# A hybrid two-block network on one core: a new order in the attention loop, a narrow normalizer and a new order in the matrix recurrences

## What is computed

```python
# mLSTM, per head: t queries, s keys
scores = einsum("tk,sk->ts", q, k) * exp(dmat - m_row)        # causal
h = (scores @ v) / maximum(abs(sum(scores, -1)), exp(-m_row)) # the normalizer
y = group_norm(h * sigmoid(og), center=True)
# SSD
y = (einsum("ln,sn,ls,sp->lp", cc, bc, lmat, xc) + xs * d_skip) * silu(z)
y = group_norm(y, 1, norm_g, center=False)
```

```python
s = einsum('qhcd,khcd->hcqk', q, k)           # two maps c per head, over 512 keys
p = softmax(s, axis=-1)
da = einsum('hqk,khv->qhv', p[:, 0] - lam * p[:, 1], v)
mx = einsum('hqm,mhd->qhd', softmax(einsum('qhd,mhd->hqm', q * 128 ** -0.5, mk)), mv)
```

## Time and profile before

| | before |
|---|---|
| median of 3 runs | 3386.85 us (3380.41 to 6549.61) |
| profiled execution | 3385.07 us, span 3383.4 us |
| instructions | 49933 |
| PE busy | 3254.1 us (96%) |
| PE weight loads | 2589.0 us (77%) |
| DVE busy | 2475.9 us (73%) |
| ACT busy | 1902.0 us (56%) |
| POOL busy | 242.4 us (7%) |
| DMA | 600.28 MB, mean 177 GB/s |

### The profile page before, as it was taken

How to read it: one execution, slowest core, us unless ns; L and a number is a source line. 1 busy time by engine, 2 the same in 40 slices (tenths; PEclk the granted TensorE clock), 3 DMA queues, 4 the chain that set the end, 5 groups by cost and what they waited for, 6 DMA issues and landing times. The chain is left out here.

```text
span 3383.4 us, 49933 instructions
## 1 busy us (share of the span) xinstructions
PE 3254.1 (96%) x19234; PEld 2589.0 (77%) x19234; DVE 2475.9 (73%) x2843; ACT 1902.0 (56%) x2145; POOL 242.4 (7%) x202
## 2 busy tenths in 40 slices
PE   8998799999999999999999998999999999899998
PEld 6876467888888888888767776788887877678886
DVE  6745759999999999999668866566536886666543
ACT  4315337777777787787547546354316635544422
POOL 0000001212212122122000000000000000000000
PEclk9999899999999999999999999999999999999999
DMA  4103259999999999999512210222322221122331
GB/s 148 64 26 109 69 206 362 371 369 364 373 360 366 374 366 360 374 360 374 205 47 89 70 60 19 85 87 94 107 92 72 73 66 42 47 84 94 100 102 67
DMA packets 118964, 600.28 MB, mean 177 GB/s; under 512 B 20738, under 2 KB 24338, under 8 KB 68402
## 3 DMA queue, kind: packets, MB, share of 16 engines
q1 hardware_dynamic: 105490, 580.64, 47.0%
q0 software_dynamic: 13312, 17.35, 2.1%
HBM read 585.77 MB, written 28.90 MB: 182 GB/s over the span
## 5 line engine op out<-in xcount | busy, mean ns | idle before, releaser
L2614 DVE TENSOR_TENSOR wl<-raw,wh 128x2048 fp32r<-128x2048 f32 x384 | 872.5, 2286 | 52.4 <-ACT wh L2543 52.4
L2543 ACT ACTIVATE wh<-raw 128x2048 fp32r<-128x2048 f32 x384 | 735.7, 1916 | 190.9 <-PE pu L2484 143.9
L2482 PE MATMUL pu<-wh,Xh 128*128 128x512 f32 x1024 | 409.7, 400 | 0.0
L2483 PE MATMUL pu<-wl,Xh 128*128 128x512 f32 x1024 | 399.7, 390 | 0.0
L2484 PE MATMUL pu<-wh,Xl 128*128 128x512 f32 x1024 | 399.2, 390 | 0.0
L4469 ACT ACTIVATE w_high<-w_raw 128x1024 fp32r<-128x1024 f32 (+1 forms) x114 | 131.2, 1151 | 319.7 <-PE acc L4441 161.1
L4516 DVE TENSOR_TENSOR w_low<-w_raw,w_high 128x1024 fp32r<-128x1024 f32 (+1 forms) x114 | 152.4, 1337 | 185.1 <-PE ps L4399 99.8
L4421 PE MATMUL ps<-x_high,w_high 128*128 128x512 f32 x656 | 255.2, 389 | 0.0
L4422 PE MATMUL ps<-x_low,w_high 128*128 128x512 f32 x656 | 255.2, 389 | 0.0
L2482 PEld LDWEIGHTS pu<-wh,Xh 128*128 128x128 f32 x1024 | 192.3, 188 | 45.6 <-issue 7.9
L2484 PEld LDWEIGHTS pu<-wh,Xl 128*128 128x128 f32 x1024 | 192.3, 188 | 42.6
(11 more groups left out here) (836 smaller groups left out, 6535.9 us busy)
## 6 DMA issues: line engine op xcount, KB each, us to landing
raw<-in_exp_w SPq DMA_DIRECT2D x384, 1024.0 KB, 7.7
w_raw<-in_w_in SPq DMA_DIRECT2D x100, 512.0 KB, 3.3
w_raw<-in_w_up SPq DMA_DIRECT2D x82, 512.0 KB, 3.7
w_raw<-in_w_down SPq DMA_DIRECT2D x32, 704.0 KB, 4.0
w_raw<-in_w_out SPq DMA_DIRECT2D x32, 384.0 KB, 3.1
kv_raw<-in_w_mem_kv SPq DMA_DIRECT2D x16, 512.0 KB, 3.7
x<-in_x SPq DMA_DIRECT2D x4, 1024.0 KB, 8.4
w_raw<-in_w_out SPq DMA_DIRECT2D x8, 512.0 KB, 4.4
```

Of the source, the lines that this page charges most:

```text
L2482: nc.tensor.matmul(o, lh[:, k, :], wh[:, m % PARTS, c], start=(m >= 8 and kh == 0 and kk == 0), stop=False)
L2483: nc.tensor.matmul(o, lh[:, k, :], wl[:, m % PARTS, c], start=False, stop=False)
L2543: nc.scalar.activation(wh[:, m % PARTS, :], raw[:, m % RAW, :], ACT.Copy).then_inc(w_high, 1)
L2614: nc.vector.tensor_tensor(wl[:, m % PARTS, :], raw[:, m % RAW, :], wh[:, m % PARTS, :], ALU.subtract).then_inc(w_low, 1)
```

## The change

It has three parts.

1. *Normalizer.* The denominators are no longer repeated over 64 partitions. `half_ones` (GpSimd makes it at the stage's start) has ones in 16 of its 48 columns; a matmul of 32 columns for each head and block of queries c puts the denominators of both heads of a pair in the partitions 32 c to 32 c + 31 of bank 0, 128 tokens wide. The bounds get the same form early (`m_bounds`, behind the first scores). ScalarE's absolute value, VectorE's maximum and its reciprocal then go over 256 elements a partition, and TensorE spreads the reciprocal over heads (`m_over`, `m_shared`) behind the first SSD sum.
2. *Order in the recurrences.* `m_rows(1)` goes ahead of the scores and sums of its step, the GLA spread ahead of the sums, `s_rows(0)` ahead of the last two sums, and in SSD step 2 the mean and `s_rows(1)` ahead of memory tile 12. Tiles 11 and 12 use bank 5. The last gate is done in halves.
3. *Attention loop.* On TensorE `scores(n + 2)` comes first, then `turn`, `mem_scores(n + 2)`, `mem_turn`, and the tile after them. `sums` writes `x_var` (first quarter) and `mem_sums` its second quarter, so `turn` waits for the gather of the step before and not for its store. One semaphore serves both sums. The scale of the scores moves into the copies that make the queries, and two small VectorE instructions a step go.

```diff
-        dn = K.sb(ctx, "dn", [P, 2, S])
+        dn = K.sb(ctx, "dn", [P, 2, P])
+        half_ones = K.sb(ctx, "half_ones", [P, 48])
+        bound_rows = K.sb(ctx, "bound_rows", [P, 2, 32])
-        kv_bank = lambda t: B[:, {10: 5, 13: 2, 14: 2, 15: 3}.get(t, 1), 0:MEM]
+        kv_bank = lambda t: B[:, {10: 5, 11: 5, 12: 5, 13: 2, 14: 2, 15: 3}.get(t, 1), 0:MEM]
...
                     for e in (0, 1):
-                        o = slice(64 * e, 64 * e + 64)
-                        mm = nc.tensor.matmul(B[o, p, j * P:S], K.c("ones", P, 0, 64), atts[q % 2][:, e, j * P:S],
-                                              start=(j == 0), stop=(j == NT - 1))
+                        for c in range(j, NT):
+                            mm = nc.tensor.matmul(B[32 * c:32 * c + 32, 0, p * P:(p + 1) * P], half_ones[:, 16 - 16 * e:48 - 16 * e],
+                                                  atts[q % 2][:, e, L[c]], start=(j == 0 and e == 0), stop=(j == c and e == 1),
+                                                  skip_group_check=True)
...
+                m_bounds()
                 for q in range(LAST):
...
+                    if q == NT - 2:
+                        m_rows(1)
                     if q + 1 < LAST:
                         m_scores(q + 1)
+                    if q == NT - 1:
+                        pe.wait_ge(l_inverse, 1)
+                        pe.wait_ge(memory.taken, MEM_TILES + 2)
+                        head_spread(B[:, 3, :], 0).then_inc(l_spread, 1)
+                        head_spread(B[:, 1, :], 1).then_inc(l_spread, 1)
+                    if q == LAST - 2:
+                        s_rows(0)
                     m_sums(q)
-                    if q == NT - 2:
-                        m_rows(1)
...
-                s_rows(0)
...
-                pe.wait_ge(m_abs, 1)
-                pe.wait_ge(em_out, 1)
-                for h in range(H):
-                    o = slice(64 * (h % 2), 64 * (h % 2) + 64)
-                    mm = nc.tensor.matmul(B[o, h // 2, :], row_of(ROW_I, h, 64), rows, start=True, stop=True)
-                mm.then_inc(em_spread, 1)
                 for q in range(LAST):
                     if q == NT:
-                        pe.wait_ge(memory.taken, MEM_TILES + 3)
+                        pe.wait_ge(memory.taken, MEM_TILES + 5)
                     s_sums(q)
...
+                    if q == 0:
+                        pe.wait_ge(m_over, 1)
+                        for p in (0, 1):
+                            for c in range(NT):
+                                mm = nc.tensor.matmul(B[:, 1 - p, L[c]], K.c("hpick", P, c), dn[:, p, :], start=True, stop=True)
+                            mm.then_inc(m_shared, 1)
...
                         dve.wait_ge(m_max, 1)
-                        step.go(nc.vector.reciprocal(dn[:, 0, :], dn[:, 0, :]))
+                        nc.vector.reciprocal(dn[:, :, :], dn[:, :, :]).then_inc(m_over, 1)
...
                     for n in range(16):
+                        if n + 2 < 16:
+                            scores(n + 2)
                         turn(n)
+                        if n + 2 < 16:
+                            mem_scores(n + 2)
                         if 1 <= n < H:
                             turn_mem(n)
-                        if n + 2 < 16:
-                            scores(n + 2)
+                        mem_turn(n)
                         if n in tile_in:
                             tile(*tile_in[n])
-                        mem_turn(n)
-                        if n + 1 < 16:
-                            mem_scores(n + 1)
...
                         if n:
-                            pe.wait_ge(a_stored, n)
+                            pe.wait_ge(a_gathered, n)
...
                         store(n)
                         mem_store(n)
-                        if n + 1 < 16:
-                            mem_exps(n + 1)
+                        if n + 2 < 16:
+                            mem_exps(n + 2)
```

More of the change, by code:

```diff
@@ L1017, in _ @@
                             nc.tensor.matmul(B[:, 2 + t, :], K.c("mean64"), ym[:, t, :], start=True, stop=True).then_inc(m_mean, 1)
+                    if q == NT - 2:
+                        s_rows(1)
+                    if q in (1, 2):
+                        for half in (0, 1):
+                            memory_tile(MEM_TILES + 2 + q, half)
                     if q == 4:
@@ L1296, in _ @@
                     if q == 0:
-                        dve.wait_ge(em_spread, 1)
+                        dve.wait_ge(bounds, 1)
                         dve.wait_ge(m_abs, 1)
-                        nc.vector.tensor_tensor(dn[:, :, :], dn[:, :, :], B[:, 0:2, :], ALU.max).then_inc(m_max, 1)
+                        nc.vector.tensor_tensor(dn[:, :, :], dn[:, :, :], B[:, 0, 2 * P:S].rearrange("p (a b) -> p a b", a=2), ALU.max).then_inc(m_max, 1)
                         dve.wait_ge(m_max, 1)
-                        step.go(nc.vector.reciprocal(dn[:, 0, :], dn[:, 0, :]))
+                        nc.vector.reciprocal(dn[:, :, :], dn[:, :, :]).then_inc(m_over, 1)
                     if q == 1:
-                        step.go(nc.vector.reciprocal(dn[:, 1, :], dn[:, 1, :]))
-                        step.all()
-                        for t in range(2):
-                            nc.vector.tensor_tensor(ym[:, t, :], dn[:, t, :], B[:, 2 + t, :], ALU.mult).then_inc(m_timed, 1)
                         dve.wait_ge(gated, 3)
                         for t in range(2):
+                            dve.wait_ge(m_shared, t + 1)
+                            nc.vector.tensor_tensor(ym[:, t, :], so[:, t, :], B[:, 1 - t, :], ALU.mult).then_inc(m_timed, 1)
+                        for t in range(2):
                             dve.wait_ge(m_timed, t + 1)
-                            nc.vector.tensor_tensor(ym[:, t, :], ym[:, t, :], so[:, t, :], ALU.mult).then_inc(m_gated, 1)
+                            nc.vector.tensor_tensor(ym[:, t, :], ym[:, t, :], B[:, 2 + t, :], ALU.mult).then_inc(m_gated, 1)
                     if q == 2:
```

95 lines of the change are left out of this document (48 added, 47 removed).

## The result

The changed kernel takes 3365.11 us (median of 5 runs, 3364.55 to 3367.50) against 3386.85 us: ratio 0.9934, 95% interval 0.9922 to 0.9946. Forecast were 3363 us and a range of 3346 to 3379. The profiled execution took 3364.91 us with a span of 3363.2 us; the earlier trace rows and the sum were made against 3385.07 and 3383.4. One of the five executions of the kernel before took 6549.61 us, for which there is no trace, and the ratio is taken without it. TensorE is busy 3246.5 us of it (97%), VectorE 2456.9 us (73%).

The account below looks back on a forecast made before the run. TensorE was taken as the bound, busy 96% of the span, with VectorE setting the pace late in the recurrences. 3385.07 less 12.2 (recurrences) and 10 (two attention loops) gave 3362.9, said as 3363 us; range 3346 to 3379.

Parts of the forecast that it names:

- A full-width step saves 0.4, the next 0.3, narrower ones less: mLSTM loop, TensorE: sums over ones as 32-column bursts save 0.4 us at full width, 0.3 us next, then less.
- First exponents: Recurrences: reordered rows, GLA spread and shorter sums start VectorE's first SSD exponents 4.7 us early, at 348.6.
- the mean and the second SSD rows stood behind memory tile 12: Recurrences, SSD: both waited behind that tile on TensorE; putting them ahead of it is worth 3.5 us.
- Tile 12 ended at 377.9; now it ends near 369.2: Recurrences: tile behind mean and rows ends near 369.2, so the fifth sum starts at 374.5 against 386.44, 11.9 us early.
- ScalarE's chain: Recurrences: ScalarE's work behind tile 12, up to the second pair's exponentials, ends last before the fifth sum; 2 us given back.
- Attention loops: Each layer: waits 13.8, drain 2.4 and slow clock 1.9 us removed, 13.2 us of new waits added; 5 us gained.
- 0.16 us of drain in each of 15 steps: Attention loop, TensorE: the new order also removes this drain, 2.4 us a layer.
- Layer 1 repeats it row for row: Attention loops: layer 1's loop matches layer 0's, so the 5 us gain counts twice, 10 us.
- The loops give nothing: Rival, attention loops: full tile steps run at TensorE's pace and waits only change names; 3373 us, chance 0.15.
- the gain is swallowed: Rival, whole kernel: later work waits on something that does not move; 3383 us, chance 0.07.
- the slow rival: Rival, attention loops: memory scores wait for the preceding step's memory exponential, over 1.5 us late; 3401 us, chance 0.05.
- Much more: Rival: waits of loop steps 7 to 11 hide behind early scores, clock stays up; 16 + 20 us, 3349 us, chance 0.13.

Follow-up runs that it names:

- order_alone: The full change with the old wide normalizer put back (64 columns of ones, maximum over 1024, two reciprocals); 3371.6 us, 0.9957 of the kernel before.
- loops_alone: The kernel before with only the attention part of the change, recurrences as before; 3377.1 us, 0.9971 of the kernel before.
- narrow_alone: The full change with the old TensorE order in the recurrences largely put back, narrow normalizer kept; 3372.6 us, 0.9963 of the kernel before.
- exponentials_first: The full change with ScalarE doing the second pair's exponentials ahead of tile 12's take, next high part and squares; 3366.6 us, 0.9932 of the kernel before.
- recurrences_alone: The kernel before with only the recurrences' part of the change, attention loops as before; 3376.8 us, 0.9969 of the kernel before.
- four_together: The full change plus second pair's exponentials first, half tile moved to step 7, second root before step 14's stores, memory values early; 3349.6 us, 0.9891 of before.

## Why the prediction was right, and where its steps were not

**Bursts.** "A full-width step saves 0.4, the next 0.3, narrower ones less" was right at most for the first. By length the saving is 0.4, 0.2, 0 and minus 0.2 us, because the two heads share a column group. From the start of the values by weights to what follows the ones, a step took 1.86, 1.44, 0.92 and 0.53 us at full clock before, and takes 1.58, 1.48, 1.14 and 0.92 us in the second pair after (1.46 and 1.36 for the first two in the first pair). So the first saves 0.3 or 0.4 us, the second next to nothing, and the narrow ones lose 0.2 and 0.4 us; over both pairs the new sums cost about 0.3 us more, where I had taken them to save over 1.4. They pay on VectorE, and ahead of the rows only because the order keeps the narrow ones behind. On TensorE's tiling rule in the Trainium skill (TensorEngine Tiling (Array Packing), Key Properties), the trace agrees in both points: the depths show the four column groups side by side, and a switch of columns has a price, 0.1 us. The prediction took the row of 0.64 us to contain it, but the part that the product ahead loses isn't in that row.

**First exponents.** 5.8 us early, not 4.7. The three orders came as worked out (the GLA spread 2.7 us early, forecast 2.6; the SSD rows 1.45 us, forecast 1.5), and the shorter sums ahead of the rows gave 0.24 us, not 0.6. The remaining 1.45 us is a term that the sum had at nothing: before, the scores and the values by weights from 343.19 took 3.20 us to the next start, where order_alone, with the same products at full clock, takes 1.76 us. These slow rows stand behind a wait of 2.47 us for the weights in three traces (before, loops_alone, narrow_alone); in the other eleven the wait is 1.55 or 1.88 us and the rows are fast. That the shorter wait is the cause is argued.

**Normalizer, mean and rows.** I had the mean's product at 363.9 in effect, and it started at 363.79, but by luck: the 1.1 us too much above cancel with 1.1 us too little on the way. The spread took 3.15 us and was not covered. Behind it the second sum, tile 11 and the third sum follow on TensorE without a pause up to the mean, for which VectorE was ready at 360.9. A smaller loss was not in the sum either: ScalarE's absolute value stands ahead of the exponentials and now waits for the last sums over ones, which come behind the SSD rows, and VectorE waits 0.54 + 0.23 us for those exponentials.

The step "the mean and the second SSD rows stood behind memory tile 12" failed. Only the mean did. The rows stood ahead of it (the trace of before has them at 373.09, tile 12 at 374.51), and the change moved them *behind* the mean, where VectorE now waits 1.03 us for them. So the exponents of the second pair came 12.8 us early, not 13.9.

That is not what made the fifth sum late (375.48, not 374.5), since ScalarE took these exponents up 3.7 us after they were done. The step that failed there is "Tile 12 ended at 377.9; now it ends near 369.2". From the mean at 363.9 this leaves 5.3 us for mean, rows and tile; they take 1.8 + 1.3 + 3.5 = 6.6 us, and tile 12 ended at 370.4, 1.2 us late. ScalarE's chain behind it was 0.2 us shorter than I had it. This 1.0 us is most of the gap from 12.2 to 10.9 us; the last gate's 0.3 us did not show. Rows ahead of the mean were not tried; they pay only where ScalarE does the exponentials first.

**ScalarE's chain.** Right: behind the end of tile 12 it ended last, and exponentials_first gives it 1.8 us, forecast 2.

**Attention loops.** The net of 5 us for layer 0 was right, but two errors of 2 us cancel in it. New waits measured in layer 0: 3 x 0.56 for memory values (forecast 3 x 0.6), 2.76 for the Silu (2.9), 1.33 + 1.13 and 0.56 + 0.99 around the first root (1.45 + 1.6 and 0.55 + 1.5), 0.56 in step 12 and 2.08 in step 15. That is 11.1 us, forecast 13.2. Not there were the waits of step 0 (0.6), step 8 (0.65), and the first output unit (0.9). Missed was step 15: I gave it a part of 1.25 us, and ScalarE's second root with its table load takes 2.08. On the other side stood 13.8 + 2.4 + 1.9 = 18.1 us. The waits taken away were 14.2 us in layer 0, and 5.0 - (14.2 - 11.1) leaves 1.9 us for the other two terms. I took the slow clock to end (1.9 us); it only moved. For the "0.16 us of drain in each of 15 steps" no row stood, and no run shows that figure; what the runs show is that steps 4 to 6 became 0.26 us shorter without a wait (6.65 to 6.39 us), which over eight tile steps is about the 1.9 us that are left. "Layer 1 repeats it row for row" holds for the waits of the change, but not for the time before, which was 1.6 us less in layer 1. There the slow stretch fell behind the wait for the Silu, where ScalarE ended last anyway (the transpose behind it waited 0.36 instead of 1.69 us), and none lay at the loop's end; hence 3.0 us there and not 5. Together 8 us, forecast 10.

**The total.** The three parts gave 18.9 us where the sum had 22.2. That the measured 3365 us is only 2 us from 3363 owes 1.3 us to stretches that the sum didn't count, and those vary by more between executions. The mechanisms held; the closeness of the total is partly luck.

**The rivals.** "The loops give nothing" falls with loops_alone, "the gain is swallowed" with the medians of recurrences_alone, the slow rival with the waits: in the change no memory scores wait. "Much more" named the waits of steps 7 to 11, and four_together shows they could be had, at 3349.6 us, but by covering them and not by the change.

## What to carry to other kernels

A new order pays by what then stands between an engine's question and its answer: put a large independent product between each transpose and its sum in exactly the steps where the other engine loads a table or does a long function, and put the short copy that gates the next step first in the other engine's order. A long wait can be worth more than its own length, since the lower clock behind it may go too. Price a short product by the distance between starts, with its neighbours, and not by its own length. Before a claim that something "stood behind", read its row; two neighbours in the new code need not have been neighbours in the old.

## What the runs showed of the hardware that I had not expected

- A burst of 32-column products lasts 0.20 us plus 0.22 us for each 128-token product of depth in the fullest column group, whatever the other groups hold: 0.64 us for 16 or 12, 0.62 us for 4, 1.52 us for 48 records.
- A change of the number of columns costs about 0.1 us between starts: 64-column sums gave way after 0.80 us with a 32-column burst behind them and after 0.70 us without, and a burst after 0.57 us, or 0.46 us with another of 32 columns behind it.
- The lower clock showed right behind long waits, but not each time: the spread of 2.05 us took 3.15 to 3.78 us after a wait of 2.17 or 2.18 us in five executions, and 2.05 us after the same wait in the six whose stage starts near 315. The scores took 2.08 instead of 1.13 us behind the wait of 2.76 us. In four_together, whose longest wait there is 1.3 us, loop 0 ran at 1.00 throughout.
- The same loop in the same code took 118.7 and 121.3 us in two executions, with the granted clock between 2060 and 2085 us at 0.97 and 0.90.
